# Sparse attention block: order of compression, gates, bias and score units

## The chip, the cores and the metric

The kernel runs on one core of one Trainium2 chip. The metric is device time in microseconds for one launch, the median of several runs.

## The reference

Two transformer blocks run one after the other on 256 tokens of width 1024. The change touches the first half of the first block only:

```
h = rms_norm(x, g);  u = h @ w_in
q, k_c, v_c, k_s, v_s, k_w, v_w, gl, b_g, c_g, x_t = split(u)
kc = gelu((blocks(k_c) + pe_k) @ wk1) @ wk2          # 15 blocks of 32 tokens, step 16; the same for v
o_c = softmax(q kc / 8 + bias) vc                   # compressed branch
o_s, o_w = the same over selected blocks and over a window
o = g0 * o_c + g1 * o_s + g2 * o_w,  g = sigmoid(gl)
y = concat(o, b_g * causal_conv(c_g * x_t)) @ w_out
```

There are 8 query heads of 64 in 2 groups, and a bias for each head and bucket of distance. At 256 tokens every block of 64 tokens is selected and the window of 512 covers everything, so the selected and the window branch both run over all earlier keys. Behind this come the residual, a feed-forward part with a short convolution, and the second block (a recurrence in chunks and 128 experts), which stay as they are.

## The kernel before

All weights come in tiles of 128x1024 fp32 (512 KB) through a ring of three slots, numbered in one stream over the whole kernel. For tile n, SyncE loads slot n mod 3, ScalarE copies it to `w_hi` in the reduced type fp32r (`split_high`, line 477), and the rest `w_lo` is subtracted (`split_low`, line 491) by VectorE for slots 0 and 1 and by GpSimd for slot 2. TensorE multiplies three products (hi x hi, hi x lo, lo x hi, line 657) and signals `tiles_used`. ScalarE may split tile n when TensorE is done with tile n - 3; SyncE may load it when n - 3 is split.

The first projection has 24 tiles (`Z1`), in a loop of 6 (`BODY`) that uses PSUM banks 0 to 5. VectorE evicts even tiles (line 1200), ScalarE odd ones (line 1754), into `z1`. Behind the loop, in this order on TensorE: gate logits (line 693, bank 6), first compression layer over 8 ring tiles `w1_cmp` with split inputs (line 704), turn of the values (line 711), turn of the hidden layer (line 717), second layer (lines 722 and 726), and six flips of the bias rows (line 737), each copied out by ScalarE (line 1771). The compression blocks are built by VectorE (line 1212) and split by ScalarE and VectorE (lines 1737 and 1171). VectorE then does the short convolution (lines 1228 to 1239).

Four score units follow: unit gi has query block gi // 2 and head group gi % 2. For units 0 and 1 there are 128 keys, for 2 and 3 there are 256. `logits` (lines 750 and 759) fills banks 0 to 4. VectorE adds the bias, takes the maximum and its negative (lines 1243 to 1245) into the one buffer `zbuf`, ScalarE takes the exponentials with their sums (line 1777), VectorE scales them by gate over sum (lines 1248 to 1254). TensorE turns them (line 768, banks 5 and 6 in turns), ScalarE copies (line 1795), TensorE multiplies by the values (`attend`, lines 789 and 792, bank 7), ScalarE copies the heads out (line 1800). TensorE has the scores of unit gi + 1 ahead of the turns of unit gi, but VectorE and ScalarE go through one unit after the other. The order on each engine is the order of the code, and semaphores tie them; nothing else plans it. After the units, `mix` is split and the output projection begins (stream position `B_OUT1`).

## Time and profile before

| | |
|---|---|
| median of 3 runs | 1732.25 us |
| lowest, highest | 1726.86, 1732.41 us |
| the profiled execution | 1732.43 us, span 1730.6 us |
| mean granted TensorE clock | 0.946 |
| busy, share of the span | TensorE 90%, VectorE 62%, ScalarE 48%, GpSimd 24% |

The span goes from the first to the last instruction of the profiled execution. A granted clock of 1.00 is 2.4 GHz, 0.50 is 1.2 GHz. The busy time of a matmul group is modelled from its starts, so a busy TensorE is not one at its peak. Idle time stands in brackets with what ended it.

### The profile page before, as it was taken

What the parts mean: (1) busy time and instruction counts of PE and PEld (TensorE: products, weight loads), DVE (VectorE), ACT (ScalarE), POOL (GpSimd) and SP (SyncE); (2) the same over time, 40 slices, a digit from 0 to 9 for tenths busy, and PEclk for the clock granted to TensorE, in tenths of its full rate; (3) what the DMA queues carried; (4) which work ended last, traced back from release to release, by engine and by line L of the source; (5) the groups of instructions that cost most, each with busy time, mean ns of one, the idle gap of its engine ahead of it and who ended that gap; (6) DMA issues with size and microseconds to landing.
All of it is one profiled execution on the core that took longest, in us unless ns stands there. A gap on an engine that the chain in (4) does not pass through costs nothing.

```text
span 1730.6 us, 32028 instructions
## 1 busy us (share of the span) xinstructions
PE 1562.0 (90%) x11368; PEld 1421.6 (82%) x11368; DVE 1076.5 (62%) x1791; ACT 838.0 (48%) x1449; POOL 411.0 (24%) x184
## 2 busy tenths in 40 slices
PE   5989879999698477877989999999999999999998
PEld 5965669999598356556989999999999988888886
DVE  3355365555527766657543889779999745545544
ACT  3445545555354211114444565666667555555554
POOL 1220112223023212101212432432222132232221
PEclk9986899999899698959999999999999999999999
DMA  6540225555154000003444555554444456665664
GB/s 224 187 147 1 68 73 188 183 184 186 66 171 146 0 1 1 2 1 98 147 137 142 182 166 189 172 181 135 143 136 133 136 192 191 196 194 185 198 194 150
DMA packets 66242, 234.70 MB, mean 136 GB/s; under 512 B 8217, under 2 KB 9257, under 8 KB 66177
## 3 DMA queue, kind: packets, MB, share of 16 engines
q1 hardware_dynamic: 65776, 232.25, 41.7%
q0 software_dynamic: 400, 1.59, 0.3%
q8 instruction: 40, 0.66, 0.2%
q14 instruction: 26, 0.20, 0.0%
HBM read 232.74 MB, written 1.06 MB: 135 GB/s over the span
## 4 chain that ended last, share of the span: by engine, by line
PE 70%; issue 15%; DVE 11%; ACT 2%; POOL 2%; DMA 0%; SPq 0%; POOLq 0%; DVEq 0%; ACTq 0%
PE psum L657 36%; PE psum L1116 20%; PE psum L933 4%; PE psum L671 4%; PE psum L1082 3%; DVE big L1365 2%; POOL w_lo L491 2%; PE psum L1056 1%; PE psum L645 1%; DVE w_lo L491 1%; DVE big L1444 1%; DVE big L1379 1%; DVE big L1434 1%; DVE big L1456 0%; PE psum L985 0%
## 5 line engine op out<-in xcount | busy, mean ns | idle before, releaser
L657 PE MATMUL psum<-x_hi,w_hi 128*128 128x256 f32 (+1 forms) x2192 | 628.3, 287 | 44.3 <-DVE x_lo L1171 23.3
L491 POOL TENSOR_TENSOR w_lo<-ring,w_hi 128x1024 fp32r<-128x1024 f32 x144 | 359.2, 2494 | 1145.1 <-ACT w_hi L477 1145.1
L657 PE MATMUL psum<-x_lo,w_hi 128*128 128x256 f32 (+1 forms) x2192 | 623.4, 284 | 0.0
L657 PE MATMUL psum<-x_hi,w_lo 128*128 128x256 f32 (+1 forms) x2192 | 623.0, 284 | 0.0
L477 ACT ACTIVATE w_hi<-ring 128x1024 fp32r<-128x1024 f32 x434 | 456.3, 1051 | 86.4 <-PE psum L657 47.3
L491 DVE TENSOR_TENSOR w_lo<-ring,w_hi 128x1024 fp32r<-128x1024 f32 x290 | 360.3, 1243 | 181.9 <-ACT w_hi L477 181.2
L657 PEld LDWEIGHTS psum<-x_hi,w_hi 128*128 128x128 f32 x2192 | 420.1, 192 | 50.6 <-issue 31.4
L657 PEld LDWEIGHTS psum<-x_hi,w_lo 128*128 128x128 f32 x2192 | 420.4, 192 | 0.0
L657 PEld LDWEIGHTS psum<-x_lo,w_hi 128*128 128x128 f32 x2192 | 417.8, 191 | 0.0
L1691 DVE TENSOR_TENSOR h_lo<-big,h_hi 128x256 fp32r<-128x256 f32 x128 | 71.7, 561 | 153.3 <-ACT h_hi L2026 153.3
L1116 PE MATMUL psum<-w_hi,h_hi 128*128 128x512 f32 x512 | 157.8, 389 | 0.0
L1116 PE MATMUL psum<-w_hi,h_lo 128*128 128x512 f32 x512 | 157.6, 389 | 0.0
L1116 PE MATMUL psum<-w_lo,h_hi 128*128 128x512 f32 x512 | 157.5, 389 | 0.0
L2026 ACT ACTIVATE h_hi<-big 128x256 fp32r (+1 forms) x128 | 53.4, 418 | 174.2 <-PE psum L1116 172.0
L1116 PEld LDWEIGHTS psum<-w_lo,h_hi 128*128 128x128 f32 x512 | 96.1, 188 | 20.0
L1116 PEld LDWEIGHTS psum<-w_hi,h_lo 128*128 128x128 f32 x512 | 96.1, 188 | 19.9
L1116 PEld LDWEIGHTS psum<-w_hi,h_hi 128*128 128x128 f32 x512 | 96.0, 188 | 20.0
L1305 DVE SCALAR_TENSOR_TENSOR big<-psum,big 128x255 f32<-128x255 f32 x88 | 42.4, 482 | 71.0 <-ACT big L1827 69.4
L2001 ACT ACTIVATE sq<-kept_sb,sq 128x128 f32<-128x128 bf16 x256 | 83.5, 401 | 4.0 <-PE psum L1082 2.0
L933 PE MATMUL psum<-big 128*128 128x128 f32 (+4 forms) x480 | 64.3, 299 | 19.4 <-DVE big L1434 7.7
L933 PEld LDWEIGHTS psum<-big 128*128 128x128 f32 (+1 forms) x480 | 55.5, 183 | 27.4 <-DVE big L1434 8.7
L1977 ACT ACTIVATE big<-psum 128x256 f32 (+1 forms) x68 | 26.2, 385 | 76.2 <-PE psum L657 76.0
(281 smaller groups left out, 1827.6 us busy)
## 6 DMA issues: line engine op xcount, KB each, us to landing
ring<-experts SPq DMA_DIRECT2D x256, 512.0 KB, 3.4
ring<-w_ffn SPq DMA_DIRECT2D x66, 512.0 KB, 3.4
ring<-w_in SPq DMA_DIRECT2D x46, 512.0 KB, 3.7
ring<-w_mid SPq DMA_DIRECT2D x24, 512.0 KB, 3.4
ring<-w_out SPq DMA_DIRECT2D x16, 512.0 KB, 3.6
ring<-w_q SPq DMA_DIRECT2D x16, 512.0 KB, 4.0
ring<-w_cmp SPq DMA_DIRECT2D x8, 512.0 KB, 3.4
big<-bias_rows POOLq DMA_DIRECT2D x1, 1536.0 KB, 8.5
```

Of the source, the lines that this page charges most:

```text
L477: act.activation(w_hi[:, n % RING, :], ring[:, n % RING, :], ACT.Copy).then_inc(high_ready, 1)
L491: eng.tensor_tensor(w_lo[:, n % RING, :], ring[:, n % RING, :], w_hi[:, n % RING, :].bitcast(F32), ALU.subtract).then_inc(low_ready2 if n ...
L657: mm = pe.matmul(dst, w[:, slot, k * P:(k + 1) * P], x[:, k, t0:t0 + width], start=(n == 0), stop=(n == 3 * len(chunks) - 1))
L671: mm = pe.matmul(psum[:, 4 + m // 2, (m % 2) * TX:(m % 2 + 1) * TX], w[:, slot, m * P:(m + 1) * P], h[:, par, :], start=False, stop=False, ...
L933: mm = pe.matmul(dst, G(a, h), r, start=True, stop=True)
L1082: mm = pe.matmul(gate_bank(q)[:, :, t], hot_1[q % 2][:, t, :].bitcast(F32), hot_2[q % 2][:, t, :], start=True, stop=True)
L1116: mm = pe.matmul(psum[:, 4 + 2 * tt + half, :], h[:, par, tt * P:(tt + 1) * P], w[:, slot, half * 512:(half + 1) * 512], start=False, stop ...
L1305: ins = dve.scalar_tensor_tensor(out=c[:, back:TX], in0=psum[:, 2 * par + half, 0:TX - back], scalar=taps[:, par, 3 * half + 2 - back:3 * ...
L1365: ins = dve.scalar_tensor_tensor(out=conv_y[:, m, :], in0=glu[:, m, t:t + T2], scalar=w, in1=conv_y[:, m, :], op0=ALU.mult, op1=ALU.add)
L1691: dve.tensor_tensor(h_lo[:, e % 2, :], act_all[:, trip(e, i, per), :], h_hi[:, e % 2, :].bitcast(F32), ALU.subtract).then_inc(coef_low, 1)
L2001: ins = act.activation(hot_2[q % 2][:, t, :], hit_2[q % 2][:, :, t], ACT.Copy, scale=chosen_t[:, 0, bass.ds(at, 1)])
L2026: act.activation(h_hi[:, e % 2, :], act_all[:, trip(e, i), :], ACT.Copy).then_inc(coef_high, 1)
```

## The change

The eight compression tiles leave the ring. SyncE loads them, unsplit, into `cmp_w`, a stretch of `big` that later holds `probs_t`, `mix` and part of `y1`, behind even projection tiles 6 to 20. The first compression layer multiplies the unsplit fp32 blocks by these raw weights, one product in place of three. Tiles 12 to 23 of the projection are written out, and between them TensorE does the gate logits (behind tile 12), the six flips (13 to 18, in banks 7 and 6), the two halves of the first compression layer (19 and 20), the turn of the hidden layer (22), the second layer and the turn of the values (23). VectorE builds the blocks beside tiles 12 to 15. All later tiles have a stream number that is 8 lower. `zbuf`, `zbuf_c` and `red` are doubled (the second `zbuf` lies in `y1`), the units are cut into steps that are ordered by hand on three engines, and the short convolution follows the last unit on VectorE.

```diff
-        zbuf = room(2, REP, TX)
-        zbuf_c = room(REP, N_CMP)
-        red = room(3, 24)
+        zbuf0 = room(2, REP, TX)
+        zbuf_c = room(2, REP, N_CMP)
+        red = room(2, 3, 24)
+        probs_at = at[0]
         probs_t = room(2, 5, REP * P)
         mix = room(KD, TX)
         y1 = room(KD, TX)
+        cmp_w = carve(probs_at, 8, TW)
+        assert probs_at + 8 * TW <= at[0]
+        zbuf = (zbuf0, y1.rearrange("p a b -> p (a b)").rearrange("p (b i k) -> p b i k", b=2, i=REP))
...
-        BIAS_BANKS = (0, 1, 2, 3, 6, 7)
+        BIAS_BANKS = (7, 6, 7, 6, 7, 6)
+        cmp_loaded = sem("cmp_loaded")
+        cmp_raw = [sem("cmp_raw_k"), sem("cmp_raw_v")]
...
-        stream = [(w1_in, Z1), (w1_cmp, 8), (w1_out, KD), (w1_ffn, 3 * NF)]
+        stream = [(w1_in, Z1), (w1_out, KD), (w1_ffn, 3 * NF)]
...
+                    for t in range(BODY, Z1):
+                        load_tile(src, t, t)
+                        if t % 2 == 0 and t < BODY + 16:
+                            j = (t - BODY) // 2
+                            sp.dma_start(cmp_w[:, j, :], w1_cmp[j]).then_inc(cmp_loaded, 16)
+                    t0 = Z1
...
+            def in1(k, i=None):
+                slot = tile_split(pe, B_IN1 + k, i)
+
+                pe.wait_ge((in1_even, in1_odd)[k % 2], trip(k // 2 + 1, i, 3))
+                project(slot, psum[:, k % BODY, 0:TX], TX, first=None if k else X_NORM0).then_inc(tiles_used, 1)
+
+            def gate_logits():
+                for qt in range(2):
+                    for k in range(KD):
+                        mm = pe.matmul(psum[:, 6, qt * 24:(qt + 1) * 24], sq[:, k, qt * P:(qt + 1) * P],
+                                       colv("gates", k * 24, (k + 1) * 24), start=(k == 0), stop=(k == KD - 1))
+                mm.then_inc(gates_sum, 1)
+
+            def bias_flip(n):
+                if n == 0:
+                    pe.wait_ge(bias_loaded, 16)
+                    pe.wait_ge(brow_ready, 1)
+                elif n == 1:
+                    pe.wait_ge(gates_ready, 1)
+                else:
+                    pe.wait_ge(bias_ready, n - 1)
                 pe.matmul(psum[:, BIAS_BANKS[n], :], const("flip"), bias_up.rearrange("p h k -> p (h k)")[:, n * 512:(n + 1) * 512],
                           start=True, stop=True).then_inc(bias_turned, 1)
+
+            def cmp_first(kv):
+                if kv == 0:
+                    pe.wait_ge(cmp_blocks, 1)
+                    pe.wait_ge(cmp_loaded, 128)
+                pe.wait_ge(bias_ready, 5 + kv)
+                for j in range(4):
+                    for r in range(4):
+                        mm = pe.matmul(psum[0:2 * N_CMP, 7 - kv, 0:2 * P], cmp_in[:, kv, 4 * j + r, :],
+                                       cmp_w[:, 4 * kv + j, 2 * r * P:2 * (r + 1) * P],
+                                       start=(j + r == 0), stop=(j + r == 6))
+                mm.then_inc(cmp_raw[kv], 1)
+
+            def cmp_turn():
+                pe.wait_ge(cmp_hid_ready, 2)
...
+            with pe.Fori(0, 2) as i:
+                for k in range(BODY):
+                    in1(k, i)
+            for k in range(2 * BODY, Z1):
+                in1(k)
+                if k == 12:
+                    gate_logits()
+                elif k < 19:
+                    bias_flip(k - 13)
+                elif k < 21:
+                    cmp_first(k - 19)
+                elif k == 22:
+                    cmp_turn()
+                elif k == 23:
+                    cmp_second()
+                    value_turn()
...
+                    pe.wait_ge(in1_even, 3 + Z1 // 2)
+                    pe.wait_ge(in1_odd, 3 + Z1 // 2)
...
-            def attend(gi):
-                qt, g = gi // 2, gi % 2
+            def turn_unit(gi):
+                qt = gi // 2
+                if gi == 0:
+                    pe.wait_ge(cmp_ready, 3)
                 for b in range(2):
                     pe.wait_ge(probs_ready, 3 * gi + b + 1)
                     for kt in range(qt + 1):
-                        turn(gi, b, lambda i: zbuf[:, b, i, kt * P:(kt + 1) * P], P)
+                        turn(gi, b, lambda i: zbuf[gi % 2][:, b, i, kt * P:(kt + 1) * P], P)
                 pe.wait_ge(probs_ready, 3 * gi + 3)
-                turn(gi, 2, lambda i: zbuf_c[:, i, :], N_CMP)
-                pe.wait_ge(turned_copied, batches[0])
-                if gi > 0:
-                    pe.wait_ge(heads_ready, gi)
+                turn(gi, 2, lambda i: zbuf_c[:, gi % 2, i, :], N_CMP)
+                return batches[0]
+
+            def attend(gi, turns):
+                qt, g = gi // 2, gi % 2
+                pe.wait_ge(turned_copied, turns)
+                if gi > 1:
+                    pe.wait_ge(heads_ready, gi - 1)
                 else:
-                    pe.wait_ge(brow_ready, 1)
+                    pe.wait_ge(vtok_ready, 1)
...
             logits(0)
-            for gi in range(4):
-                if gi < 3:
-                    logits(gi + 1)
-                attend(gi)
+            logits(1)
+            turns = turn_unit(0)
+            logits(2)
+            attend(0, turns)
+            turns = turn_unit(1)
+            attend(1, turns)
+            logits(3)
+            for gi in (2, 3):
+                turns = turn_unit(gi)
+                attend(gi, turns)
...
+            with dve.Fori(0, 2) as i:
                 for k in range(BODY):
-                    split_low(dve, B_IN1 + k + 2, i)
-                    if k % 2 == 0:
-                        dve.wait_ge(tiles_used, i * BODY + (B_IN1 + k + 1))
-                        dve.tensor_copy(z1[:, i * BODY + k, :], psum[:, k, 0:TX]).then_inc(in1_even, 1)
+                    in1(k, i)
             dve.wait_ge(first_loaded, 16)
+            for k in range(2 * BODY, Z1):
+                in1(k)
+                if k == 12:
+                    dve.wait_ge(in1_odd, 3 + 4)
+                    dve.wait_ge(in1_even, 3 + 4)
+                if k < 16:
+                    for n in (2 * (k - 12), 2 * (k - 12) + 1):
+                        ins = cmp_block(n)
+                    if k == 15:
+                        ins.then_inc(cmp_blocks, 1)
+            dve.wait_ge(cmp_sum, 1)
+            dve.tensor_copy(k_cmp[0:HD, :], psum[0:HD, 6, 0:N_CMP]).then_inc(cmp_ready, 1)
+            dve.tensor_copy(k_cmp[HD:P, :], psum[HD:P, 6, N_CMP:2 * N_CMP]).then_inc(cmp_ready, 1)
+            dve.tensor_copy(v_cmp[0:N_CMP, :], psum[0:N_CMP, 6, 64:64 + P]).then_inc(cmp_ready, 1)
+            dve.wait_ge(vtok_sum, 1)
+            dve.tensor_copy(v_tok.rearrange("p a b c -> p (a b c)"), psum[:, 7, :]).then_inc(vtok_ready, 1)
...
+            TURNS = (0, 0, 3, 6)
+
+            def unit_max(gi):
...
+                    if gi >= 2 and b == 0:
+                        dve.wait_ge(turned, TURNS[gi])
...
+            unit_max(0)
+            unit_max(1)
+            unit_gated(0)
+            unit_max(2)
+            unit_gated(1)
+            unit_max(3)
+            unit_gated(2)
+            unit_gated(3)
+            short_conv()
...
+            def cmp_gelu(kv):
+                act.wait_ge(cmp_raw[kv], 1)
+                act.activation(cmp_act[0:2 * N_CMP, kv, :], psum[0:2 * N_CMP, 7 - kv, 0:2 * P],
+                               ACT.Gelu_apprx_tanh).then_inc(cmp_hid_ready, 1)
+
+            with act.Fori(0, 2) as i:
                 for k in range(BODY):
-                    split_high(act, B_IN1 + k + 2, i)
-                    if k % 2:
-                        act.wait_ge(tiles_used, i * BODY + (B_IN1 + k + 1))
-                        act.activation(z1[:, i * BODY + k, :], psum[:, k, 0:TX], ACT.Copy).then_inc(in1_odd, 1)
-            act.wait_ge(gates_sum, 1)
-            act.activation(gates, psum[:, 6, 0:48].rearrange("p (a b) -> p a b", a=2), ACT.Sigmoid).then_inc(gates_ready, 1)
-            act.wait_ge(cmp_blocks, 1)
-            high_x(X_CMP, cmp_quarter)
-            for kv in range(2):
-                for j in range(4):
-                    split_high(act, B_CMP + 4 * kv + j + 2)
-                act.wait_ge(tiles_used, B_CMP + 4 * (kv + 1))
-                act.activation(cmp_act[0:2 * N_CMP, kv, :], psum[0:2 * N_CMP, kv, 0:2 * P],
-                               ACT.Gelu_apprx_tanh).then_inc(cmp_hid_ready, 1)
+                    in1(k, i)
+            for k in range(2 * BODY, Z1):
+                in1(k)
+                if k == 13:
+                    act.wait_ge(gates_sum, 1)
+                    act.activation(gates, psum[:, 6, 0:48].rearrange("p (a b) -> p a b", a=2), ACT.Sigmoid).then_inc(gates_ready, 1)
+                if 14 <= k < 20:
+                    n = k - 14
+                    act.wait_ge(bias_turned, n + 1)
+                    act.activation(bias_t.rearrange("p h k -> p (h k)")[:, n * 512:(n + 1) * 512], psum[:, BIAS_BANKS[n], :],
+                                   ACT.Copy).then_inc(bias_ready, 1)
+                elif 20 <= k < 22:
+                    cmp_gelu(k - 20)
...
+            unit_exp(0)
+            unit_exp(1)
+            unit_turned(0)
+            unit_exp(2)
+            unit_head(0)
+            unit_turned(1)
+            unit_head(1)
+            unit_exp(3)
+            unit_turned(2)
+            unit_head(2)
+            unit_turned(3)
+            unit_head(3)
```

## Rows read from the trace of the kernel before

**Rows 1.** Windows: stretch, length, busy time of each engine, granted clock, DMA share, GB/s.

```profile
24.00:94.69 70.69, 70.37 (x576) 70.37 (x577) 26.65 (x32) 28.71 (x36) 19.74 (x8) 0.96 0.57 181
94.69:129.58 34.89, 27.71 (x162) 20.80 (x161) 19.59 (x35) 17.32 (x26) 7.09 (x3) 0.80 0.42 137
129.58:192.25 62.67, 52.83 (x192) 31.57 (x192) 32.11 (x77) 31.63 (x117) 0.00 (x0) 0.73 0.00 1
```

**Rows 2.** Timeline of TensorE, compression stretch: start, duration, engine, line, tiles, [idle before, releaser].

```profile
94.69 4.48 PE L693 MATMUL psum<-big,sq 128*128 128x24 f32 x32
101.88 0.42 PE L704 MATMUL psum<-w_hi,x_hi 128*30 128x256 f32 x1 [2.71 <-DVE x_lo L1171]
...
116.86 0.60 PE L711 MATMUL psum<-kept_sb,big 128*128 128x128 f32 x4
119.89 0.43 PE L717 MATMUL psum<-kept_sb,big 30*128 30x30 f32 x4 [2.43 <-ACT big L1763]
...
122.20 6.61 PE L737 MATMUL psum<-big 128*128 128x512 f32 x12
```

**Rows 3.** Timeline of ScalarE: evictions of two odd projection tiles.

```profile
89.30 0.39 ACT L1754 ACTIVATE big<-psum 128x256 f32 x1 [1.87 <-PE psum L657]
...
94.98 0.38 ACT L1754 ACTIVATE big<-psum 128x256 f32 x1 [1.87 <-PE psum L657]
```

**Rows 4.** Windows around the falls and returns of the granted clock.

```profile
97.60:107.40 9.80, 7.09 (x34) 5.93 (x34) 4.93 (x10) 3.60 (x8) 2.37 (x1) 0.50 0.17 56
129.58:134.80 5.22, 4.73 (x38) 4.45 (x39) 4.09 (x12) 3.45 (x13) 0.00 (x0) 1.00 0.01 3
134.80:162.10 27.30, 25.95 (x71) 15.19 (x70) 13.40 (x33) 10.45 (x45) 0.00 (x0) 0.50 0.00 0
179.60:186.20 6.60, 4.64 (x20) 3.56 (x20) 3.84 (x10) 5.40 (x20) 0.00 (x0) 0.51 0.00 1
```

**Rows 5.** Timeline of TensorE: a sum of squares, eight plain fp32 matmuls, 256 columns.

```profile
219.25 3.62 PE L645 MATMUL psum<-sq,kept_sb 128*128 128x256 f32 x16
```

**Rows 6.** Timeline of TensorE in the score units, full clock.

```profile
129.58 2.02 PE L750 MATMUL psum<-big 64*128 64x128 f32 x16 [0.78 <-ACT big L1771]
...
162.94 3.72 PE L750 MATMUL psum<-big 64*128 64x256 f32 x16
166.50 0.96 PE L759 MATMUL psum<-big 64*128 64x15 f32 x8
...
169.64 1.07 PE L768 MATMUL psum<-kept_sb,big 128*128 128x128 f32 x8 [1.07 <-ACT big L1795]
...
172.32 3.66 PE L789 MATMUL psum<-big 128*64 128x512 f32 x8 [0.68 <-ACT big L1795]
175.91 1.07 PE L792 MATMUL psum<-big 15*64 15x512 f32 x2
```

**Rows 7.** Timeline of VectorE in the score units.

```profile
130.85 0.69 DVE L1243 SCALAR_TENSOR_TENSOR big<-psum,big 128x512 f32<-128x512 f32 x1 [0.89 <-PE psum L750]
...
157.60 1.23 DVE L1243 SCALAR_TENSOR_TENSOR big<-psum,big 128x1024 f32<-128x1024 f32 x1 [5.79 <-PE psum L768]
...
160.19 1.22 DVE L1243 SCALAR_TENSOR_TENSOR big<-psum,big 128x1024 f32<-128x1024 f32 x1
```

**Rows 8.** Groups of ScalarE, score units: count, busy us, mean ns, idle before.

```profile
L1777 ACT ACTIVATE big<-big 128x256 f32<-128x256 f32 x16 | 7.9, 495 | 0.0
L1795 ACT ACTIVATE big<-psum 128x512 f32<-128x512 f32 x12 | 6.9, 596 | 8.0 <-PE psum L768 7.9
L1777 ACT ACTIVATE big<-big 128x128 f32<-128x128 f32 x16 | 6.2, 389 | 1.8 <-DVE big L1245 1.8
```

**Rows 9.** Timeline of VectorE: first and last of 14 short convolution instructions.

```profile
122.92 1.20 DVE L1228 TENSOR_TENSOR big<-big 128x1024 f32<-128x1024 f32 x1
...
128.74 1.23 DVE L1239 TENSOR_TENSOR big<-big 128x1024 f32<-128x1024 f32 x1
```

**Rows 10.** Timeline of TensorE, first gate tile behind the recurrence.

```profile
800.57 0.55 PE L657 MATMUL psum<-x_hi,w_hi 128*128 128x256 f32 x1 [2.34 <-POOL w_lo L491]
```

More of the change, by code:

```diff
@@ L683, in _ @@
             norm_pe(0, TX, 6)
-            with pe.Fori(0, Z1 // BODY) as i:
-                for k in range(BODY):
-                    slot = tile_split(pe, B_IN1 + k, i)
-                    pe.wait_ge((in1_even, in1_odd)[k % 2], i * 3 + (k // 2 + 1))
-                    project(slot, psum[:, k, 0:TX], TX, first=None if k else X_NORM0).then_inc(tiles_used, 1)
-            for qt in range(2):
-                for k in range(KD):
-                    mm = pe.matmul(psum[:, 6, qt * 24:(qt + 1) * 24], sq[:, k, qt * P:(qt + 1) * P],
-                                   colv("gates", k * 24, (k + 1) * 24), start=(k == 0), stop=(k == KD - 1))
@@ L695, in _ @@
-            mm.then_inc(gates_sum, 1)
-            pe.wait_ge(x_split, 4 * X_CMP + 4)
-            for kv in range(2):
-                for j in range(4):
-                    slot = tile_split(pe, B_CMP + kv * 4 + j)
-                    for r in range(4):
-                        for n, (w, x) in enumerate(((w_hi, x_hi), (w_hi, x_lo), (w_lo, x_hi))):
-                            mm = pe.matmul(psum[0:2 * N_CMP, kv, 0:2 * P], x[:, 4 * kv + j, r * 2 * N_CMP:(r + 1) * 2 * N_CMP],
-                                           w[:, slot, 2 * r * P:2 * (r + 1) * P],
-                                           start=(j + r + n == 0), stop=(j + r + n == 8))
-                    mm.then_inc(tiles_used, 1)
@@ L719, in _ @@
-            mm.then_inc(cmp_hid_sum, 1)
-            pe.wait_ge(cmp_hid_ready, 3)
-            for c in range(2):
-                pe.matmul(psum[:, 5, 0:2 * N_CMP], colv("w2k", c * P, (c + 1) * P), cmp_hid[:, 0, c, :],
-                          start=(c == 0), stop=(c == 1))
-            for g in range(N_KV):
-                for c in range(2):
-                    mm = pe.matmul(psum[0:N_CMP, 5, 64 + g * HD:64 + (g + 1) * HD],
-                                   cmp_hid[:, 1, c, g * N_CMP:(g + 1) * N_CMP], colv("w2v", c * HD, (c + 1) * HD),
-                                   start=(c == 0), stop=(c == 1))
@@ L729, in _ @@
-            mm.then_inc(cmp_sum, 1)
-            pe.wait_ge(bias_loaded, 16)
-            pe.wait_ge(gates_ready, 1)
-            pe.wait_ge(brow_ready, 1)
-            for n in range(6):
+            def in1(k, i=None):
[8 more added lines that the diff above has]
+                mm.then_inc(gates_sum, 1)
@@ new lines, in cmp_turn, with cmp_second @@
+            def cmp_turn():
+                pe.wait_ge(cmp_hid_ready, 2)
+                for kv in range(2):
+                    for c in range(2):
+                        mm = pe.transpose(psum[:, 7, (2 * kv + c) * 32:(2 * kv + c) * 32 + 2 * N_CMP],
+                                          cmp_act[0:2 * N_CMP, kv, c * P:(c + 1) * P], const("ident")[0:2 * N_CMP, 0:2 * N_CMP])
+                mm.then_inc(cmp_hid_sum, 1)
+            def cmp_second():
+                pe.wait_ge(cmp_hid_ready, 3)
+                for c in range(2):
+                    pe.matmul(psum[:, 6, 0:2 * N_CMP], colv("w2k", c * P, (c + 1) * P), cmp_hid[:, 0, c, :],
+                              start=(c == 0), stop=(c == 1))
+                for g in range(N_KV):
+                    for c in range(2):
+                        mm = pe.matmul(psum[0:N_CMP, 6, 64 + g * HD:64 + (g + 1) * HD],
+                                       cmp_hid[:, 1, c, g * N_CMP:(g + 1) * N_CMP], colv("w2v", c * HD, (c + 1) * HD),
+                                       start=(c == 0), stop=(c == 1))
+                mm.then_inc(cmp_sum, 1)
@@ L1194, in _, with in1, cmp_block @@
             dve.sem_inc(in1_even, 3)
-            with dve.Fori(0, Z1 // BODY) as i:
+            def in1(k, i=None):
+                split_low(dve, B_IN1 + k + 2, i)
+                if k % 2 == 0:
+                    dve.wait_ge(tiles_used, trip(B_IN1 + k + 1, i))
+                    dve.tensor_copy(z1[:, trip(k, i), :], psum[:, k % BODY, 0:TX]).then_inc(in1_even, 1)
+            blocks = [(kv, g, half) for kv in range(2) for g in range(N_KV) for half in range(2)]
+            def cmp_block(n):
+                kv, g, half = blocks[n]
+                q = slice(half * HD, (half + 1) * HD)
+                src = z1[q, ZKC + 2 * kv + g, half * 16:half * 16 + 16 * N_CMP].rearrange("p (n r) -> p r n", r=16)
+                return dve.tensor_tensor(cmp_in[q, kv, :, g * N_CMP:(g + 1) * N_CMP], src,
+                                         colv("pe", kv * 16, kv * 16 + 16)[q].unsqueeze(2).to_broadcast([HD, 16, N_CMP]),
+                                         ALU.add)
```

108 lines of the change are left out of this document (40 added, 68 removed).

## The prediction

> **What bounds the kernel now.** I read the windows of the stretch that the change touches first. They cut the profile at the last matmul of the first projection, at the first score matmul and at the last head copy. TensorE is busy in 70.4 of 70.7 us of the projection, 27.7 of 34.9 us of the compression stretch and 52.8 of 62.7 us of the score units, at granted clocks of 0.96, 0.80 and 0.73 [rows 1]. So the projection has no room, and the 97.6 us behind it are slow for three reasons: engines wait for each other, TensorE runs at its lower level (0.50 of full, 1.2 GHz), and the work is small. The timeline of TensorE shows the order of the 34.9 us: gate logits, a wait of 2.71 us for the split of the blocks, 96 compression products, value turns, the turn of the hidden layer behind a wait of 2.43 us, the bias flips, and scores at 129.58 [rows 2]. The chain of waits of this stretch puts most of its time down to "issue" and I don't use it.
>
> **Part 1: first projection, compression, gates, bias.** The 24 projection tiles keep their cost: two tiles lie 5.68 us apart, 2.84 each [rows 3]. Twelve of them run as before. Behind tiles 12 to 23 small work is put between tiles, so what used to wait now waits beside a tile. What TensorE still does outside its 24 tiles:
> - Gate logits: 4.5 us as now [rows 2]. The clock fell inside them, at 97.6, and was back at 107.4 [rows 4], though TensorE waited 2.7 us of that. I expect the same fall, with tile 13 behind it at the low level: about 5 us of full-rate work done at half rate, half of it extra, 2.5 us. Bounds: 0 (no fall) and 3.
> - Six flips: a 128x512 fp32 matmul takes about 3.66/4 = 0.9 us at the high level [rows 6], so 5.4 us, against 6.61 us now with a low clock at their start [rows 2].
> - Compression: 96 split products become 32 plain fp32 matmuls, 30 columns held and 256 moving. No row shows that shape in plain fp32. The nearest is the 128x256 fp32 sum of squares, 8 matmuls in 3.62 us, 0.45 each [rows 5], 14.5 us for 32. Below, the split products bound it (96 of them filled the 15.0 us from 101.88 to 116.86, part at the low clock; three at the projection's pace of 2.84/24 = 0.118 us are 0.35 us, 11.4 us in all [rows 2, 3]). Above, the 64x256 fp32 scores do (8 in 3.72 us, 0.465 each, 14.9 us [rows 6]). I take 14.5. On TensorE alone this edit is no gain; what it removes is 8 splits on ScalarE, VectorE and GpSimd, the split of the blocks (the 2.71 us wait) and the ring's turns.
> - Turn of the hidden layer and second compression matmuls: 2.3 us from 119.89 to the first flip [rows 2]. The turn now lies ahead of tile 23, but the copy it feeds stands behind ScalarE's eviction of tile 23 (0.4 us, [rows 3]), so TensorE still waits at the second matmuls. With the value turns (0.6 us, [rows 2]) 3.3 us.
> Sum: 4.5 + 2.5 + 5.4 + 14.5 + 3.3 = 30.2 us in place of 34.9, a gain of 4.7 us.
>
> What I cost at nothing here. ScalarE gets a sigmoid, six copies of 0.6 us [rows 8] and two GELUs between splits, VectorE eight block adds; in a stretch of tiles each has over 1.5 us idle of every 2.84 us (28.7 and 26.7 us busy of 70.7, [rows 1]), and from tile 13 on every tile lasts 0.9 to 7 us longer. If that cover is gone a tile starts late by the length of the piece, 1 to 2 us once. SP's queue gets 8 extra 512 KB loads behind even tiles 6 to 20: DMA share was 0.57 at 181 GB/s [rows 1]. One and a half times that is 0.86 in the densest part. At 181/0.57 = 318 GB/s a 512 KB load fills the engines for 1.6 us, so a ring load may land that much later; ScalarE was idle 1.87 us for TensorE before an eviction [rows 3], so it did not wait for loads there. The new waits of TensorE for flips, gates and raw weights have their releasers a tile or more ahead; everything behind such a wait on its queue is the projection, and ScalarE, VectorE and the ring would stop with it.
>
> **Part 2: the score units.** Durations at the high level, per step: scores of one branch 1.0 us at 128 keys and 1.86 at 256, compressed scores 0.96, one turn 0.54, attend 2.9 in units 0 and 1 and 3.66 + 1.07 = 4.7 in units 2 and 3 [rows 6]. VectorE: bias, maximum and sign of one branch take 2.59 us at 256 keys (157.60 to 160.19) and two passes of 0.69 with the sign, 1.53, at 128 [rows 7]; one such pass and three instructions on four columns make the gating, 1.2 and 1.7, and the compressed branch 0.6 and 0.95, read as estimates from these. ScalarE: four exponentials of 0.39 or 0.50, 1.54 and 1.97 us, compressed 1.2, copies 0.6 [rows 8]. The order before, laid out on three queues with the clock low where it was (5 to 32.5 and 50 to 56.5 us behind the first score, [rows 4]), gives 64.9 us; the trace has 62.7, so I take 2.2 off each layout.
>
> The new order has, at the high level throughout, this chain: first scores 1.1; VectorE's maxima of units 0 and 1 and gating of unit 0 to 12.0; turn 12.6; scores of unit 2 14.5; maxima of unit 2 20.4; gating of unit 1 23.7; turn and copy 25.4; attend(1) 28.4; scores of unit 3, queued behind it, 30.2; its maxima 36.1; gating of unit 2 and turns 41.4; copy and attend(2) 46.9; turns of unit 3 50.7; attend(3) 55.4; copy 56.1. So the doubled buffers overlap ScalarE and VectorE, but two things come late: VectorE does unit 3's maxima ahead of unit 2's gating, and TensorE does unit 2's scores ahead of attend(0). The old order at the high level comes to 50.7 in the same layout: the reordering itself does not pay where TensorE is fast. It pays where TensorE is slow. With the clock low from 3 to 32 us, TensorE's steps in the chain in that time (0.5, 1.9, 2.9, 1.9) double, 63.3 us, less 2.2 is 61.1: a gain of 1.6 us. Ends: 53.9 (never low) and 80.6 (low from 3 us to the end).
>
> The short convolution (122.92 to 129.97, 7.05 us, [rows 9]) leaves the place beside the flips and follows the last gating. There it lies beside TensorE's turns and attend(3): 11.3 us from the last gating to the last head copy in the layout. Hidden; without that cover it costs up to 7.
>
> **Part 3: tile numbers.** Eight tiles fewer shift the slot of every later tile by one modulo 3, so other tiles get GpSimd's 2.4 us split. In the feed-forward loop no tile waits for its split now; no row of mine bounds the new place's slack there, so the ends are wider. At 800.57 TensorE waited 2.34 us for such a split [rows 10]; that tile goes to VectorE, whose split is about half as long (it handles 1024 columns in 1.2 us in [rows 7]). I take a gain of 1.2 us; the ends are 2.3 us gained and 2 us lost.
>
> Sum: 4.7 + 1.6 + 1.2 = 7.5 us off the profiled execution's 1732.43 us (span 1730.6), which is 0.2 above the median 1732.25: 1724.9 us.
>
> **The clock rule.** The granted clock was at its full level from 129.58 to 134.8, with TensorE busy 4.7 of 5.2 us, and then at 0.50 (1.2 GHz) from 134.8 to 162.1 with TensorE busy nearly throughout [rows 4]; the gate logits ran without a gap when it fell at 97.6 [rows 2, 4]. The Trainium skill ("TensorE: Matmul & The Clock Gate", section "What's actually happening") says that the low level is the default, that an idle stretch brings it and sustained activity releases it. By that rule the gate logits and the dense first 7 us of units would stay high; the trace speaks against it. The result that the rule would give is rival A.
>
> **Rivals.**
> A. TensorE stays at the high level through gates and units. For: part 1 ends in dense tiles, and scores of two units stand back to back. Against: the falls at 97.6 and 134.8 came in small matmuls without a long wait [rows 2, 4]. Gains 7.2 + 8.8 + 1.2 = 17.2: 1715 us.
> B. TensorE stays low through the units, because turns, scores and waits come in smaller groups. For: it was low for 27 us of them. Against: it came back at 162.1 in the middle of them [rows 4]. Layouts: low to 46 us gives 67.0 after the 2.2, a loss of 4.3, total gain 1.6; low to 60 gives 73.6, and from there on the whole change is slower by over 5 us; low to the end 80.6, 17.9 - 5.9 = 12 us slower: 1744 us.
> C. The interleaving loses its cover: a split or a landing is late at several of the twelve tiles, 1.5 us each at four tiles, 6 us. 1731 us.
> D. The change keeps part 1's gain and the later stages, which sit at the edge of the clock's two levels, move by some us either way; the three runs before differ by 5.5 us. It widens the range only.
>
> **Chances.** Forecast 0.42 (own range 1719 to 1731), A 0.20, B 0.18 (half of it slower), C 0.20. A measurement of this kernel tells about 0.3%, 5.2 us, from no change. Faster: most of the forecast and A, 0.56. Same: C, the rest of the forecast and the mild half of B, 0.27. Slower: strong B and mishaps of D, 0.17. Range for 8 in 10: 1713 to 1738.
>
> **What would show it.** Right: no w_cmp splits on any engine; the last projection matmul near 119 to 122 and the first score at 124 to 126; compression matmuls in two groups of some 7.2 us; the stretch from first score to last head copy 58 to 64 us with one long low stretch; scores of unit 3 behind attend(1), and VectorE idle some 6 us before its maxima; the short convolution ended before the last head copy. Wrong: waits of over 1 us of TensorE for w_lo between tiles 6 and 23; first score before 122 or after 128; units above 68 us or below 56.

## The result, and the profile after

The changed kernel takes 1737.7 us (median of 12 runs, 1734.0 to 1745.9) against 1732.3 us of the kernel before in the same session. The ratio is 1.0044, 95% interval 1.0028 to 1.0060: it is slower by 0.44%, or 7.6 us by the ratio. Timed again beside other kernels it had 1.0054 (1.0031 to 1.0076). The forecast was 1724.9 us, faster. The profiled execution took 1735.2 us (span 1733.4, mean granted clock 0.947).

The surprise is in the order of things. In the profile the changed stretch is faster, and the loss lies in stages that the change did not mean to touch. These are the windows that answer to [rows 1], with the same columns, cut at the last projection matmuls, the first score and the split of `mix`:

```profile
24.00:120.50 96.50, 95.86 (x688) 85.04 (x688) 33.70 (x40) 35.22 (x47) 19.64 (x8) 0.95 0.51 177
120.50:122.95 2.45, 1.82 (x18) 1.38 (x17) 0.42 (x3) 1.83 (x3) 0.00 (x0) 1.00 0.61 221
122.95:185.04 62.09, 49.01 (x193) 29.81 (x192) 38.52 (x92) 31.21 (x118) 0.00 (x0) 0.78 0.00 0
```

TensorE is busy in 95.9 of the first 96.5 us: the small work between the tiles costs only itself. The small groups, by the timeline of TensorE:

```profile
63.92 3.79 PE L701 MATMUL psum<-big,sq 128*128 128x24 f32 x32
71.87 1.02 PE L713 MATMUL psum<-big 128*128 128x512 f32 x2
...
94.16 7.12 PE L723 MATMUL psum<-big 128*30 128x256 f32 x32
```

The first score is at 122.95 (129.58 before). The units, on the same timeline:

```profile
122.95 2.05 PE L785 MATMUL psum<-big 64*128 64x128 f32 x16
...
132.78 2.04 PE L803 MATMUL psum<-kept_sb,big 128*128 128x128 f32 x8 [2.88 <-DVE big L1306]
...
136.06 7.19 PE L785 MATMUL psum<-big 64*128 64x256 f32 x16
143.04 1.72 PE L794 MATMUL psum<-big 64*128 64x15 f32 x8
144.70 3.67 PE L830 MATMUL psum<-big 128*64 128x512 f32 x4
...
155.30 3.72 PE L785 MATMUL psum<-big 64*128 64x256 f32 x16
...
164.79 4.84 PE L803 MATMUL psum<-kept_sb,big 128*128 128x128 f32 x20 [4.98 <-DVE big L1306]
...
182.65 1.07 PE L833 MATMUL psum<-big 15*64 15x512 f32 x2
```

The same 16 score matmuls take 7.19 us at 136.06 and 3.72 us at 155.30: the granted clock is 0.51 from 128.4 to 148.9 (the low level, 1.2 GHz) and 0.99 from there to 162.6 (2.4 GHz). From first score to the end of the last attend it is 60.8 us (62.0 before), and the kernel leads by 7.9 us at the split of `mix` (185.0 against 192.9). Then the lead goes. The table cuts each profile at VectorE's first split of the inputs of the next projection, its first step of the recurrence, its first max8 and its copy of the keys:

| stretch, us | before | after |
|---|---|---|
| split of `mix` at | 192.9 | 185.0 |
| to the feed-forward part | 48.4 | 47.0 |
| feed-forward part | 216.2 | 218.6 |
| second input projection | 88.7 | 87.0 |
| recurrence and middle tiles | 275.5 | 280.3 |
| to the first max8 | 123.9 | 124.7 |
| top-k beside the query and first expert tiles | 196.9 | 202.4 |
| experts, up to the first `h_lo` | 230.6 | 230.9 |

One cut of the table does not stand at the same place of the work in both kernels. VectorE's first step of the recurrence comes one projection tile (2.8 us) earlier against ScalarE's and TensorE's work in the changed kernel, as its distance to VectorE's next step that waits for ScalarE shows, 9.3 us before and 12.2 after:

```profile
546.17 1.18 DVE L1389 TENSOR_SCALAR big<-big,kept_sb 128x272 f32<-128x272 f32 x4
...
555.50 0.73 DVE L1396 TENSOR_SCALAR big<-big 128x1088 f32<-128x1088 f32 x1 [5.88 <-ACT big L1879]
```

```profile
537.58 1.18 DVE L1456 TENSOR_SCALAR big<-big,kept_sb 128x272 f32<-128x272 f32 x4
...
549.76 0.73 DVE L1463 TENSOR_SCALAR big<-big 128x1088 f32<-128x1088 f32 x1 [3.94 <-ACT big L1971]
```

Cut at the later step, the second input projection takes 98.0 us before and 99.2 after, and the stretch of recurrence and middle tiles 266.2 and 268.1.

Three views show where the new slots tell. First, the row at 800.57 in [rows 10] has become one long wait, here with VectorE's and GpSimd's rows around it:

```profile
799.47 0.55 PE L665 MATMUL psum<-x_hi,w_hi 128*128 128x256 f32 x1 [7.05 <-DVE w_lo L497]
...
791.12 6.95 DVE L1573 RECIPROCAL big<-big 128x1088 f32<-128x1088 f32 x1
798.10 1.23 DVE L497 TENSOR_TENSOR w_lo<-ring,w_hi 128x1024 fp32r<-128x1024 f32 x1
...
794.70 2.34 POOL L497 TENSOR_TENSOR w_lo<-ring,w_hi 128x1024 fp32r<-128x1024 f32 x1 [11.62 <-ACT w_hi L483]
```

The tile's split has moved from GpSimd to VectorE, where it stands behind a reciprocal of 6.95 us. Second, the feed-forward part, as VectorE's groups of one line, before and after:

```profile
L1315 DVE TENSOR_TENSOR big<-big 128x256 f32<-128x256 f32 x22 | 9.4, 426 | 1.5 <-ACT big L1830 0.7
```

```profile
L1382 DVE TENSOR_TENSOR big<-big 128x256 f32<-128x256 f32 x22 | 44.0, 2000 | 1.5 <-ACT big L1922 0.7
```

The same instruction takes 2.0 us instead of 0.43, since it now begins 0.6 us after GpSimd's split and ends just behind it:

```profile
307.68 2.40 POOL L497 TENSOR_TENSOR w_lo<-ring,w_hi 128x1024 fp32r<-128x1024 f32 x1 [6.17 <-ACT w_hi L483]
...
308.28 2.08 DVE L1382 TENSOR_TENSOR big<-big 128x256 f32<-128x256 f32 x1
```

Most of this is slack, but at the end of the part TensorE waits for what follows from it, `h_lo`, 2.76 us in place of 0.83. Before and after:

```profile
430.82 0.36 PE L671 MATMUL psum<-h_hi,w_hi 128*128 128x256 f32 x1 [0.83 <-DVE h_lo L1319]
```

```profile
419.46 2.36 POOL L497 TENSOR_TENSOR w_lo<-ring,w_hi 128x1024 fp32r<-128x1024 f32 x1 [6.09 <-ACT w_hi L483]
...
420.13 1.98 DVE L1382 TENSOR_TENSOR big<-big 128x256 f32<-128x256 f32 x1
...
423.16 0.36 PE L679 MATMUL psum<-h_hi,w_hi 128*128 128x256 f32 x1 [2.76 <-DVE h_lo L1386]
```

Third, the top-k stage, TensorE's wait in it and what led to it:

```profile
1068.66 3.76 POOL L497 TENSOR_TENSOR w_lo<-ring,w_hi 128x1024 fp32r<-128x1024 f32 x1 [6.13 <-ACT w_hi L483]
...
1067.93 2.29 DVE L1656 TENSOR_TENSOR big<-big 128x2048 f32<-128x2048 f32 x1
1070.25 3.25 DVE L497 TENSOR_TENSOR w_lo<-ring,w_hi 128x1024 fp32r<-128x1024 f32 x1
...
1073.63 0.38 PE L665 MATMUL psum<-x_hi,w_hi 128*128 128x256 f32 x1 [3.68 <-DVE w_lo L497]
```

GpSimd's split (2.4 us by itself) waits for VectorE's 2.29 us instruction, then VectorE's own split (1.2 us by itself) waits for GpSimd's, and TensorE waits 3.68 us for VectorE's. Over the stage its waits for splits are 6.1 us, where the kernel before has 2.7.

### The profile page after: what moved, and what is told of

Same layout as the page of the kernel before. It is cut to its first block, busy times and chain, and to the rows that moved or that the text cites. A ratio compares the mean times of both kernels' runs of the same rounds, so it can differ in the third digit from the quotient of the medians.

```text
span 1733.4 us, 31801 instructions
## 1 busy us (share of the span) xinstructions
PE 1565.2 (90%) x11336; PEld 1422.6 (82%) x11336; DVE 1104.4 (64%) x1781; ACT 826.9 (48%) x1437; POOL 405.6 (23%) x182
## 3 DMA queue, kind: packets, MB, share of 16 engines
q0 software_dynamic: 400, 1.59, 0.2%
## 4 chain that ended last, share of the span: by engine, by line
PE 67%; DVE 17%; issue 9%; ACT 4%; POOL 2%; DMA 0%; DVEq 0%; SPq 0%; ACTq 0%; POOLq 0%
PE psum L665 30%; PE psum L1160 20%; PE psum L977 3%; PE psum L1126 3%; DVE big L1382 3%; DVE w_lo L497 2%; DVE big L1372 2%; PE psum L653 2%; POOL w_lo L497 1%; ACT w_hi L483 1%; DVE big L1432 1%; PE psum L1100 1%; PE psum L723 1%; DVE sq L1202 1%; PE psum L830 1%
## 5 line engine op out<-in xcount | busy, mean ns | idle before, releaser
L665 PE MATMUL psum<-x_hi,w_hi 128*128 128x256 f32 (+1 forms) x2192 | 632.9, 289 | 50.7 <-DVE x_lo L1215 23.3
L497 POOL TENSOR_TENSOR w_lo<-ring,w_hi 128x1024 fp32r<-128x1024 f32 x142 | 353.9, 2492 | 1150.7 <-ACT w_hi L483 1150.7
L497 DVE TENSOR_TENSOR w_lo<-ring,w_hi 128x1024 fp32r<-128x1024 f32 x284 | 356.2, 1255 | 228.0 <-ACT w_hi L483 227.3
L483 ACT ACTIVATE w_hi<-ring 128x1024 fp32r<-128x1024 f32 x426 | 447.3, 1050 | 67.9 <-PE psum L665 55.7
L977 PE MATMUL psum<-big 128*128 128x128 f32 (+4 forms) x480 | 60.4, 287 | 16.9 <-DVE big L1511 7.0
L977 PEld LDWEIGHTS psum<-big 128*128 128x128 f32 (+1 forms) x480 | 51.6, 171 | 24.8 <-issue 6.8
L1432 DVE SCALAR_TENSOR_TENSOR big<-big 128x272 f32<-128x272 f32 x120 | 60.5, 547 | 0.0
```

Source lines behind the costliest of these rows:

```text
L483: act.activation(w_hi[:, n % RING, :], ring[:, n % RING, :], ACT.Copy).then_inc(high_ready, 1)
L497: eng.tensor_tensor(w_lo[:, n % RING, :], ring[:, n % RING, :], w_hi[:, n % RING, :].bitcast(F32), ALU.subtract).then_inc(low_ready2 if n ...
L665: mm = pe.matmul(dst, w[:, slot, k * P:(k + 1) * P], x[:, k, t0:t0 + width], start=(n == 0), stop=(n == 3 * len(chunks) - 1))
L977: mm = pe.matmul(dst, G(a, h), r, start=True, stop=True)
L1432: ins = dve.scalar_tensor_tensor(out=conv_y[:, m, :], in0=glu[:, m, t:t + T2], scalar=w, in1=conv_y[:, m, :], op0=ALU.mult, op1=ALU.add)
```

## The experiments

Theory: the slowdown comes from the tile numbers alone. Eight tiles fewer move GpSimd's share from tiles B_OUT1, +3, ... to +2, +5, .... Rival: it comes from the new first part and units. All kernels were timed in five rounds except where a single run is named; ratios are to the kernel before on the same chip.

**The old assignment, in whole and in part.** A function decides which tiles are GpSimd's, and the waits count accordingly.

```
+        TURN = [(0, 2), (B_OUT1, 0)]
+        def on_pool(n):
+            return n % RING == [s for a, s in TURN if n >= a][-1]
...
-            if n % RING == 2:
+            if on_pool(n):
```

> The changed kernel, with GpSimd taking slot 0 in place of slot 2 from the output projection's first tile on, so that every later tile is split by the engine that split it before the change. The two first stages stay as changed. Theory S (the shift of the slots by one modulo 3 gives the gain back later): the 8 us by which the units end earlier stay, 1724 to 1728 us, 9 to 12 us under the changed kernel. Rival T (later stages only lose because they start at another moment against the clock's falls and returns): no difference, 1735 to 1740 us.

Measured: 1725.8 us, 0.9993 (0.9972 to 1.0015).

> The kernel of e1_realign a second time, beside the others and for a second profile. If the length of TensorE's low stretch in the units is a matter of the single execution, it differs from e1_realign's (0.50 from 129 to 176) by several us here; if the kernel sets it, it is the same within 1 us. Time: ratio 0.997 to 1.002.

Measured, on another chip: 1728.1 us, 0.9984 (0.9961 to 1.0006).

The reverse, the kernel before with the shift alone (`TURN = [(0, 2), (B_OUT1, 1)]` in its own numbers):

> The kernel before, with one edit: from the output projection's first tile on GpSimd takes slot 1 in place of slot 2, so every later tile is split by the engine that splits it in the changed kernel. Theory S: 9 to 12 us slower than before, 1741 to 1745 us. Rival T: within 3 us of before, 1729 to 1736 us.

Measured: 1744.3 us, 1.0086 (1.0064 to 1.0108). The shift of the slots, with no other edit, costs 15 us. The theory holds from both sides: the slots make the slowdown. With the old ones the time is that of the kernel before, though, and not the gain that parts 1 and 2 had promised.

Half of the tiles each, with the border three tiles ahead of the query tiles:

```
+        TURN = [(0, 2), (B_OUT1, 0), (B_Q - 3, 2)]    # early tiles as before
+        TURN = [(0, 2), (B_Q - 3, 0)]                 # late tiles as before
```

> The changed kernel with the old engine for each tile restored from the output projection to the second block's output projection only; queries, keys and experts stay shifted. Theory S, from the drift of equal instructions between the two traces (6.3 us of the lead lost up to 876 us, 5.8 us behind it): about 5 us under the changed kernel, 1732 to 1734 us. Rival T: no difference, 1735 to 1740 us.

Measured: 1731.8 us, 1.0018 (0.9999 to 1.0036).

> The changed kernel with the old engine for each tile restored only from three tiles before the query projection on (queries, keys, experts). Theory S: about 5.5 us under the changed kernel, 1731 to 1734 us, most of it between 945 and 1130 us, where the top-k instructions lie between splits. Rival T: no difference, 1735 to 1740 us.

Measured: 1740.0 us, 1.0045 (1.0022 to 1.0068). In the profiles the top-k stage lasts 202.3 us in the first and 196.9 in the second. The first kernel came as expected. The second did not: it has the ratio of the change (1.0044 and 1.0054), though its top-k stage is 5.5 us shorter. Its profile gives that back elsewhere, with 67.4 us in the units (the change 60.8) and 283.7 in the recurrence and middle tiles (280.3). So the early half shows by itself (0.003 between e3_realign_early and the change) and the late one only on top of it (0.003 between e3_realign_early and the two realigned runs). Each ratio is sure to about 0.002, so neither share is firm.

**The third assignment.** `TURN = [(0, 2), (B_OUT1, 1)]` in the changed kernel.

> As e1_realign, but from B_OUT1 on GpSimd has the tiles of slot 1: the third of the three possible assignments (before: the tiles B_OUT1, +3, ...; the change: +2, +5, ...; here +1, +4, ...). Theory (the order of VectorE's other work in the top-k stage and in the middle projections fits only the old assignment): ratio 1.003 to 1.010, with the top-k stage, max8 to key copy, over 201 us against 197. Rival (the change's assignment is merely the worst of three): ratio 0.998 to 1.002 and 197 us or less.

Measured: 1736.6 us, 1.0031 (1.0012 to 1.0050). The ratio is as the theory said, its place is not: the top-k stage has 197.0 us, but the stretch of recurrence and middle tiles has 280.3, with the same wait of 7.0 us as the change. In the middle both other assignments give the tile behind the reciprocal to VectorE; in the top-k stage only the change's is bad. The third one loses most in a place of its own: up to the later step of the recurrence its second input projection takes 102.2 us, in place of 98.0 and 99.2.

**The place of the splits in the top-k stage.** VectorE's splits there stand at every 2100 passed elements of its other work. The counter now starts half way.

```
-            passed = [0]
+            passed = [1050]
```

> e3_realign_early with the change's slots in the top-k stage, and VectorE's splits in that stage half a step earlier in its own work (the counter that places them starts at 1050 of 2100). Theory (in the top-k stage the shift hurts because VectorE's splits stand where the old numbering wanted them): the stage from first max8 to the copy of the keys comes down from 202.3 us to 197 to 200, and TensorE's wait of 3.7 us for a split of VectorE goes. Rival (the loss is in GpSimd's splits of other tiles, not in VectorE's order): 202 us or more.

> f2_other_order, with the old assignment of the engines, and the same half step in the top-k stage. Theory (place of the splits and slot have to fit each other): the stage stays at 196.9 us or becomes up to 4 us longer. Rival (earlier splits are better for any assignment): 194 to 196 us.

Measured, one run each: with the change's slots the stage falls from 202.3 to 195.3 us (kernel 1727.3 us); with the old slots it rises from 196.9 to 200.2 (kernel 1710.0, which has the third order of the units described below). Slot and place have to fit each other. TensorE's waits in the stage, first with the change's slots as they were, then with the earlier splits:

```profile
PE psum L665 <- DVE w_lo L497: 4.6, 5, 3.7
PE psum L665 <- POOL w_lo L497: 1.5, 2, 1.3
```

```profile
PE psum L676 <- DVE w_lo L505: 1.1, 4, 0.4
PE psum L676 <- ACT big L2071: 1.0, 1, 1.0
```

The same edit in the changed kernel, and with the early tiles on their old engines besides:

> The changed kernel with its own slots everywhere; only VectorE's splits in the top-k stage stand half a step earlier (counter from 1050 of 2100). Theory (the slots hurt in two places, 5.4 us in the top-k stage by the place of the splits, and 2 to 5 us ahead of it): the stage lasts 195 to 196 us, the ratio is 1.0005 to 1.003, where the change has 1.0044 and 1.0054. Rival (the top-k stage is all of it): 0.998 to 1.0005. Rival (the time is given back later): 1.004 or more.

> The kernel of g3_splits_earlier timed in rounds: old assignment of the engines up to the query tiles, the change's slots and earlier splits behind them. Theory: 7 us below e3_realign_early (1.0018), ratio 0.9965 to 0.999, and 2 to 5 us below h1_change_earlier. Rival (the assignment ahead of the top-k stage costs nothing): the same as h1_change_earlier within 1 us.

Measured: 1733.5 us, 1.0030 (1.0009 to 1.0051), and 1727.1 us, 0.9980 (0.9959 to 1.0001). In both profiles the top-k stage has 195.3 us, as the theory said, and the first ratio lands at the edge of its range. The step between the two, 0.0050 or 8.7 us, is what the assignment costs ahead of the top-k stage, more than the 2 to 5 us that I expected. It is sure to about 5 us; the two profiles differ by 6.2.

**The order of the units.** On the realigned kernel, first the old order on all three engines (what is left of the change is its first part), then a third order.

```
-            unit_max(0); unit_max(1); unit_gated(0); unit_max(2); ...
+            for gi in range(4):
+                unit_max(gi)
+                unit_gated(gi)
```

> The changed kernel with the splits of all tiles from B_OUT1 on back on their old engines (as in e1_realign) and with the score units in their old order: each unit from maxima to head copy before the next. What is left of the change is the first part (compression, gates and flips between projection tiles) and the short convolution behind the units. Theory 1 (the new order of the units costs what the first part gains): the units last 60 to 64 us as before, the first score is at 122 to 124, so the ratio to the kernel before is 0.996 to 0.998, and it is 2 to 6 us faster than the same kernel with the new order. Rival (the order of the units does not matter, and the 6 us lead is lost to TensorE's clock, which stays low longer whenever the units start behind dense tiles): the units last 67 to 70 us in the old order too, ratio 0.999 to 1.001, as e1_realign.

Measured: 1729.1 us, 0.9971 (0.9945 to 0.9996). The ratio is the theory's, but its mechanism is not shown: the units last 66.5 us in this profile too, with the clock low from 128 to 169.

```
             turns = turn_unit(1)
+            logits(3)
             attend(1, turns)
-            logits(3)
...
-            unit_exp(0); unit_exp(1); unit_turned(0); unit_exp(2); unit_head(0); ...
+            unit_exp(0); unit_turned(0); unit_exp(1); unit_head(0); unit_turned(1); unit_exp(2); ...
```

> As e1_realign, with a third order of the units: VectorE goes through one unit after the other, ScalarE has the exponentials of unit u + 1 between the turns and the head copy of unit u, and TensorE has the scores of unit 3 ahead of attend(1). Laid out on three queues with the durations of the profile before, it ends 4 to 11 us ahead of the change's order at a clock like the one before, 1 us ahead if the clock is low for 48 us. Theory (VectorE's maxima ahead of gatings hold the chain up in the change's order): ratio 0.993 to 0.997, units of 55 to 64 us. Rival (the clock's low stretch decides, not the order): within 1 us of e1_realign and f1_first_part, ratio 0.998 to 1.001.

Measured: 1718.7 us, 0.9933 (0.9908 to 0.9958), the theory. Its units lasted 44.0 us in the profile, less than the 55 to 64 expected; but the profiled execution, 1707.4 us, is the fastest of its ten, and a full clock is part of that. Here is TensorE in it, where VectorE goes through one unit after the other and the granted clock is 1.00 from 134 on:

```profile
130.59 2.91 PE L813 MATMUL psum<-kept_sb,big 128*128 128x128 f32 x12
133.96 3.72 PE L795 MATMUL psum<-big 64*128 64x256 f32 x16 [0.46 <-DVE big L1307]
...
143.23 3.72 PE L795 MATMUL psum<-big 64*128 64x256 f32 x16
...
147.67 1.93 PE L840 MATMUL psum<-big 128*64 128x512 f32 x4
...
154.71 3.65 PE L840 MATMUL psum<-big 128*64 128x512 f32 x8 [0.68 <-ACT big L1876]
```

The third order with the change's slots:

> The changed kernel with its own tile numbers (GpSimd has slot 2), and the third order of the units, of f2_other_order. If the slots and the order are separate causes that add up, it stands to f2_other_order (0.9933) as the change (1.0044) to e1_realign (0.9993 and 0.9984): 0.9985 to 1.001. Rival (a shorter low stretch in the units shifts the later clock pattern so that the slots no longer matter): 0.993 to 0.996.

Measured: 1725.5 us, 0.9966 (0.9941 to 0.9992). It lies between theory and rival and above f2_other_order by 0.0033, where the theory had 0.0055; the interval reaches into both ranges, so this run alone does not tell them apart, and two ratios sure to 0.0025 each do not even prove that the slots still cost something. In its profile the top-k stage lasts 202.3 us again. The units last 61.8 us there, no less than in the change, with the clock at 0.51 for 44.3 of them; that execution took 1739.2 us, near the slowest of its twelve. In the four profiles of the third order the units last 44.0 (twice), 50.3 and 61.8 us.

The change as it is, for a second profile of its units:

> The changed kernel as it is, beside the others, with a second profile. In six profiles of kernels that have the same instructions and the same slots up to the end of the units, the units lasted 60.8 us in one (the change's own) and 67.7 to 68.6 in the three others with its order. If the single execution sets the length of TensorE's low stretch, this profile is more likely to show 68 us and a lead of under 1 us at the split of mix (191 to 192.5 us against 192.9 before). If it is set by the kernel as a whole, it shows 60.8 us and 185 us again. Ratio 1.002 to 1.007 either way.

Measured: 1739.6 us, 1.0054 (1.0031 to 1.0076), units of 60.6 us and the split of `mix` at 184.4. The less likely answer came, and f4_realign_again had given the same one: 67.4 us in both profiles of that kernel. Over all profiles of this order the stretch from first score to the end of the last attend is 67.4 us (five profiles of four kernels), 60.6 to 60.8 (the two of the change) and 59.3 to 59.4 (three). The instructions in it are the same. So a kernel repeated its length both times that it was profiled twice, and kernels that differ only behind the units do not share one. What differs is the granted clock, here in e1_realign, where it stays low from 128.9 to 176 though TensorE is busy in 39.7 of 47.1 us:

```profile
128.90:176.00 47.10, 39.70 (x112) 24.71 (x111) 25.05 (x63) 23.21 (x96) 0.00 (x0) 0.50 0.00 0
176.00:190.70 14.70, 12.59 (x43) 4.52 (x41) 8.69 (x19) 4.24 (x8) 0.00 (x0) 0.96 0.01 1
```

**All that helps together**: early tiles on their old engines, the change's slots and earlier splits in the top-k stage, the third order.

> h2_early_realigned_earlier with the third order of the units. If the parts add up: f2_other_order (0.9933) less 1.6 us of the top-k stage (195.3 us against 196.9), ratio 0.991 to 0.993. Rival (a shorter unit stretch moves the later clock pattern to a worse one): 0.994 or more.

Measured: 1712.1 us, 0.9900 (0.9868 to 0.9933). The parts add up, slightly better than expected and within the noise; it beats the kernel before by 17 us and the change by 26. In its profile the units last 50.3 us and the top-k stage 195.3; it is the version to keep.

## Why the prediction was wrong

The ratios split the change into its three parts. At 1732 us, 0.001 is 1.7 us. Each ratio is sure to about 4 us, so the +3.0 of part 2 is not told from zero, and the +10.5 of part 3 is.

| part | forecast, us | from the runs, us |
|---|---|---|
| 1, first projection to first score | -4.7 | -5.0 (f1_first_part, 0.9971) |
| 2, order of the units | -1.6 | +3.0 (to the mean of the two realigned runs, 0.9989) |
| 3, tile numbers | -1.2 | +10.5 (to the mean of the two runs of the change, 1.0049) |

**Part 1 was right.** In the profile the first score is 6.6 us earlier, the forecast said 4.7. The -5.0 of the table holds the later place of the short convolution as well, and a stretch of units that was 4.4 us longer than before in that profile. Compression took 7.12 us a half (7.2 forecast), the flips 1.02 each (0.9), the gate logits 3.79 (4.5), with the clock at 0.66 from 66 to 70. The wait ahead of the second matmuls is 0.6 us where I had left it over 1. Splits, loads and new waits hid as costed: from 24 us on TensorE had no wait for a weight split or a load in the projection, rival C did not come.

**Part 2 was right in the one profile and wrong on the whole.** Its chain came as laid out: maxima of unit 3 behind an idle 7.9 us of VectorE, scores of unit 3 behind attend(1), the convolution ended at 178, ahead of the last head copy at 183.8, and 61.4 us to the end of that copy for 61.1. But that number hung on one low stretch of 29 us, copied from the profile before. The profile has two, 20.5 us and 6.8 (0.51 from 128.4 to 148.9, 0.52 from 162.6 to 169.4), so the agreement to 0.3 us is in part luck. Of ten profiles of this order five had a low stretch of 47 us, which is rival B in part, and their units lasted 5.3 us longer than those of the kernel before. What the layout did say, that the old order is better at full clock (50.7 against 56.1 us), was the warning: it called for another order. The third one is faster in the timed runs (0.9933 for 0.9989), and in two profiles, with the clock high nearly throughout, its units lasted 44.0 us.

**Part 3 is the step that failed.** I costed the shift from one row [rows 10] as a gain of 1.2 us, with ends of 2.3 us gained and 2 lost. I priced the split by VectorE's own duration (1.2 us against 2.4), at one row, and left out what stands ahead of it on VectorE's queue, what it does to GpSimd's and VectorE's instructions beside it, and every other row. The shift measured 10.5 us lost in the table and 15 in e2_shift_only. In the profiles, six with the change's slots and ten with the old ones, it has these pieces:
- In the top-k stage 202.3 us in place of 196.9, in every profile where the place of VectorE's splits was left alone (five with the change's slots in that stage). It is the largest piece and the surest, since g3_splits_earlier moved it by that place alone.
- In the feed-forward part 220.0 us in the mean of six against 217.9 in the mean of ten, ranges that overlap. What does not overlap is the wait for the last `h_lo`, 2.7 to 2.8 us in all six and 0.83 in all ten. Inside the loop my "no tile waits for its split" held, and yet VectorE lost 35 us of slack to GpSimd.
- At the row of [rows 10] the waits for splits add up to 7.0 us, behind the reciprocal of 6.95 us, after 5.4 before (2.34, 1.51 and 1.59). Five of the ten profiles with the old slots have 7.3 us there as well (2.3 and 5.0), so the one row that I read decides little either way.
- Between the start of the second input projection and the later step of the recurrence 99.1 us in the mean against 98.3, and from there to the branch 269.3 against 265.8. From the first of the waits above to the branch the change takes 2.0 us more than the kernel before, 1.6 of them the waits. The recurrence itself, from the later step to the first of these waits, takes the same time in both, at a slightly different granted clock:

```profile
555.50:798.22 242.72, 172.90 (x1691) 134.72 (x1689) 165.05 (x272) 48.87 (x91) 36.21 (x18) 0.83 0.02 6
```

```profile
549.76:792.42 242.66, 176.19 (x1691) 138.44 (x1689) 162.51 (x271) 49.12 (x91) 38.26 (x18) 0.81 0.02 5
```

Over all profiles that part spreads from 237.3 to 244.3 us with the old slots and from 242.5 to 246.4 with the change's. Whether the slots have a part in this spread is open.

With 1 us more in the other stretches the means sum to 13 us, between the 10.5 of the table and the 15 of e2_shift_only.

The error was one of reading. "The round robin moves by one" is an edit of every later stage, and I looked for its effect where a wait already stood, at one row. The rows to read were VectorE's long instructions (over 2 us) and which tile's split stands behind each, and the VectorE instructions that fall beside a split of GpSimd's. The Trainium skill ("SBUF — State Buffer", section "Terms") says that VectorE and GpSimd share a port pair as an exclusive lock, held for a whole instruction, and that the loser blocks. The trace agrees: the feed-forward instruction, which reads two tensors of SBUF, takes 2.0 us in place of 0.43 beside GpSimd's split. It did not stand in the prediction, where it would have spoken against this part.

## What to carry to other kernels

Where work is dealt to engines in turn, a change in the number of items is a change of every later stage: pin the assignment to the consumer, or re-read the queue ahead of each item. Choose the order of a small-matmul stretch by its length at full clock, and do not copy the low stretch from the profile before: with the same instructions it differed from kernel to kernel. Before comparing a stage of two profiles, see that its cuts stand at the same place of the work on every engine. A gain in one stage of a single profile is worth what the medians say, here 5 us of part 1 (sure to about 4) and nothing of part 2.

## What the runs showed of the hardware

A VectorE tensor_tensor on 128x256 fp32 took 2.0 us in place of 0.43 when it fell beside GpSimd's 2.4 us split, and GpSimd's split took 3.76 us when VectorE's 2.29 us instruction was ahead of it: each waits for the other to finish. TensorE's clock stayed at 0.50 for 47 us with TensorE busy in 39.7 of them, and in the change's two profiles of the same instructions it was back after 20.5 us. In ten profiles of these instructions the units came in three lengths (59.3, 60.7, 67.4 us) rather than spread out. A lower granted clock does not always cost: the recurrence took 242.7 us at 0.83 and at 0.81.
